# Attention: four of nine key-tile pairs' prob_hi added up on GpSimd, and two maximum banks read by one instruction

## The reference

```
s = einsum('bqkgd,bskd->bkgqs', qblk, k)
p = softmax(s, axis=-1)
return einsum('bkgqs,bskd->bqkgd', p, v)
```

## Time and profile before

| | |
|---|---|
| runs | 1791.49, 1791.6, 1797.52 us; median 1791.6 |
| profiled execution, span | 1794.3 us (its own time isn't given separately) |
| instructions | 22369 |
| attention, first score to last copy | about 322 to 1173 us |

### The profile page before, as it was taken

The page is one execution under the profiler, slowest core; times in us unless marked ns, Lnnn a source line. Parts: engine busy times, 40 slices in busy tenths (PEclk is TensorE's granted clock), DMA queues, the critical chain, the costliest instruction groups (busy, mean ns, idle before and its releaser), DMA issues. The chain is left out here.

```text
span 1794.3 us, 22369 instructions
## 1 busy us (share of the span) xinstructions
PE 1661.6 (93%) x7388; PEld 1314.8 (73%) x7388; DVE 1014.5 (57%) x1451; ACT 832.4 (46%) x1042; POOL 505.2 (28%) x281
## 2 busy tenths in 40 slices
PE   7798885899999999999999999979999969988998
PEld 1487773677777777777777777768888848877886
DVE  1468776687787777778778778530000322254553
ACT  1454532466666766667666666711111132331111
POOL 0032332255445545545444544510000000000000
PEclk9799996799999999999999999989999979999999
DMA  6655445300000000000000000083231035658761
GB/s 223 250 179 169 158 144 133 128 15 23 21 23 16 21 23 15 24 22 15 23 21 16 22 21 23 6 223 124 105 117 47 28 145 199 188 163 231 215 219 74
DMA packets 120466, 171.01 MB, mean 95 GB/s; under 512 B 16065, under 2 KB 82625, under 8 KB 117858
## 3 DMA queue, kind: packets, MB, share of 16 engines
q1 hardware_dynamic: 111874, 147.30, 25.5%
q0 software_dynamic: 8544, 23.07, 4.0%
HBM read 119.89 MB, written 50.46 MB: 95 GB/s over the span
## 5 line engine op out<-in xcount | busy, mean ns | idle before, releaser
L826 DVE TENSOR_REDUCE chunk_max<-max_ps 128x1 f32<-128x512 f32 (+1 forms) x640 | 395.4, 635 | 66.3 <-PE max_ps L892 60.6
L755 POOL TENSOR_TENSOR prob_lo<-prob,prob_hi 128x1024 fp32r<-128x1024 f32 x128 | 306.5, 2395 | 417.3 <-ACT prob L788 417.3
L787 ACT ACTIVATE prob_hi<-s_ps 128x1024 fp32r<-128x1024 f32 x288 | 294.9, 1024 | 229.2 <-PE s_ps L910 229.1
L788 ACT ACTIVATE prob<-s_ps 128x1024 f32<-128x1024 f32 x288 | 293.6, 1019 | 0.0
L892 PE MATMUL max_ps<-k_hi,blk_q_hilo 128*128 128x512 f32 (+1 forms) x640 | 248.1, 390 | 30.3 <-DVE chunk_max L826 12.9
L909 PE MATMUL s_ps<-blk_q_hilo,k_hi 128*128 128x512 f32 x576 | 233.3, 405 | 1.1 <-DVE blk_q_negm L842 0.8
L910 PE MATMUL s_ps<-blk_q_negm,k_lo 65*128 65x512 f32 x576 | 229.3, 398 | 0.0
L930 PE MATMUL hi_ps<-prob_hi,v_hl 128*128 128x512 f32 x576 | 227.6, 395 | 1.5 <-POOL prob_lo L755 1.0
L932 PE MATMUL lo_ps<-prob_lo,v_one 128*128 128x512 f32 x576 | 228.6, 397 | 0.0
L931 PE MATMUL lo_ps<-prob_hi,zero_one 128*128 128x512 f32 x576 | 227.0, 394 | 0.0
L848 DVE TENSOR_TENSOR prob_lo<-prob,prob_hi 128x1024 fp32r<-128x1024 f32 x160 | 197.1, 1232 | 28.4 <-ACT prob L788 28.4
(11 more groups left out here) (169 smaller groups left out, 2508.0 us busy)
## 6 DMA issues: line engine op xcount, KB each, us to landing
tab<-in_dft POOLq DMA_DIRECT2D x16, 1024.0 KB, 7.1
w_mod<-in_w_mod SPq DMA_DIRECT2D x6, 2048.0 KB, 17.4
x<-in_x SPq DMA_DIRECT2D x8, 1024.0 KB, 5.5
h_scratch<-h_hi SPq DMA_DIRECT2D x8, 1024.0 KB, 4.2
h_scratch<-h_lo SPq DMA_DIRECT2D x8, 1024.0 KB, 6.5
q_scratch<-q_hilo SPq DMA_DIRECT2D x16, 512.0 KB, 3.2
blk_q_hilo<-q_scratch SPq DMA_DIRECT2D x32, 256.0 KB, 2.8
hh<-h_scratch SPq DMA_DIRECT2D x4, 2048.0 KB, 10.5
```

Source lines behind the costliest of these rows:

```text
L755: nc.gpsimd.tensor_tensor(prob_lo[slot3(j)][:], prob[slot3(j)][:], prob_hi[slot3(j)][:].bitcast(F32), ALU.subtract).then_inc(s_lo_pool, 1)
L787: nc.scalar.activation(prob_hi[slot3(j)][:], s[:], ACT.Exp)
L788: nc.scalar.activation(prob[slot3(j)][:], s[:], ACT.Exp).then_inc(s_exp, 1)
L826: last = nc.vector.reduce_max(chunk_max[:, qt, kc:kc + 1], bank[:, 0:MAX_CHUNKS[kc]], X_AXIS)
```

## The change

prob_hi of the pairs 0, 1, 3 and 4 is no longer multiplied by zero_one on TensorE. GpSimd adds these four 128 x 1024 tiles up in p_sum (three additions, add), VectorE adds its two halves (fold), ScalarE rounds the result (sum_high), VectorE forms the rest (sum_low), and TensorE multiplies both by zero_one in the last key tile. Exponentials that would overwrite a summed prob_hi wait for its addition. prob_lo is written over prob. Pair 3's lo moves from VectorE to GpSimd, pair 4's from GpSimd to VectorE.

The two maximum banks become one tile max_ps. A use fills both by two matmuls, one reduction reads both, there are 10 uses per block, and s_mfree starts at 1. A use comes after the first scores step and, where MAX_AT has 2, after the first pv step. In the diff, lines with # name the engine; the moved combine (lines 771 and 774 with their waits) is unchanged.

```diff
-MAX_CHUNKS = [512, 512, 512, 512, 256]
-MAX_USES = QB // P * len(MAX_CHUNKS)
-MAX_AT = (4, 4, 3, 4, 3, 2, 0, 0, 0)
-LO_AFTER = (2, 0, 1, 0, 1, 0, 0, 0, 0)
+QT = QB // P
+CHUNK = 512
+CHUNKS = SEQ // CHUNK
+MAX_USES = QT * CHUNKS // 2 + QT // 2
+MAX_AT = (1, 2, 2, 2, 2, 1, 0, 0, 0)
...
-POOL_LO = (0, 2, 4, 6)
+POOL_LO = (0, 2, 3, 6)
+SUMMED = (0, 1, 3, 4)
+FOLD_AT = 6
+ADDS = len(SUMMED) - 1
+
+def max_pair(u):
+    if u < QT * CHUNKS // 2:
+        qt, half = divmod(u, CHUNKS // 2)
+        return [(qt, 2 * half * CHUNK, CHUNK), (qt, (2 * half + 1) * CHUNK, CHUNK)]
+    qt = 2 * (u - QT * CHUNKS // 2)
+    return [(qt, SEQ, CTX), (qt + 1, SEQ, CTX)]
...
-        prob_lo = [sb(f"prob_lo{i}", [P, 2 * QB], F32R) for i in range(3)]
+        prob_lo = [nc.alloc_sbuf_tensor_at(f"prob_lo{i}", [P, 2 * QB], F32R, offset=prob_at + 8 * QB * i)
+                   for i in range(3)]
...
+        p_sum = sb("p_sum", [P, 2 * QB])
+        p_sum_hi = sb("p_sum_hi", [P, QB], F32R)
+        p_sum_lo = sb("p_sum_lo", [P, QB], F32R)
...
-        max_ps = [ps(f"max_ps{i}", [P, QB]) for i in range(2)]
+        max_ps = ps("max_ps", [P, 2, QB])
...
# GpSimd
+            def add(b, i):
+                j = SUMMED[i + 1]
+                if i == 0:
+                    pool.wait_ge(s_sumlo, b + 1)
+                else:
+                    pool.wait_ge(s_acc, b * ADDS + i)
+                pool.wait_ge(s_exp, b * PAIRS + (j + 3))
+                before = prob_hi[slot3(SUMMED[0])] if i == 0 else p_sum
+                nc.gpsimd.tensor_tensor(p_sum[:], before[:].bitcast(F32), prob_hi[slot3(j)][:].bitcast(F32),
+                                        ALU.add).then_inc(s_acc, 1)
...
             def body(b, slot, kvh, next_kvh):
+                add(b, 0)
+                lo(b, 2)
+                lo(b, 3)
+                add(b, 1)
+                add(b, 2)
+                lo(b, 6)
+                if next_kvh is not None:
+                    lo(b + 1, 0)
+                combine(b, slot)
...
# ScalarE, exponentials and body
+                if j >= 3 and j - 3 in SUMMED:
+                    act.wait_ge(s_acc, b * ADDS + max(SUMMED.index(j - 3), 1))
...
+            def sum_high(b):
+                act.wait_ge(s_fold, b + 2)
+                act.wait_ge(s_losum, b + 1)
+                nc.scalar.activation(p_sum_hi[:], p_sum[:, 0:QB], ACT.Copy).then_inc(s_sumhi, 1)
...
+                sum_high(b)
                 if next_kvh is not None:
                     exponentials(b + 1, 1 - slot, 0)
                 evacuate(b, slot)
...
# VectorE
-            dve.sem_inc(s_mfree, 2)
+            dve.sem_inc(s_mfree, 1)
...
             def reduce(b, slot, u):
-                qt, kc = divmod(u, len(MAX_CHUNKS))
-                bank = max_ps[(slot * (MAX_USES + 1) + u) % 2]
+                (qt, key0, width), (qt1, _, _) = max_pair(u)
+                chunk = key0 // CHUNK
+                out = chunk_max[:, qt, chunk:chunk + 2] if qt == qt1 else chunk_max[:, qt:qt + 2, chunk]
                 dve.wait_ge(s_mfull, b * (MAX_USES + 1) + (u + 1))
-                last = nc.vector.reduce_max(chunk_max[:, qt, kc:kc + 1], bank[:, 0:MAX_CHUNKS[kc]], X_AXIS)
+                last = nc.vector.reduce_max(out, max_ps[:, :, 0:width], X_AXIS)
...
+            def fold(b):
+                dve.wait_ge(s_acc, b * ADDS + ADDS)
+                nc.vector.tensor_tensor(p_sum[:, 0:QB], p_sum[:, 0:QB], p_sum[:, QB:2 * QB], ALU.add).then_inc(s_fold, 1)
+
+            def sum_low(b):
+                dve.wait_ge(s_sumhi, b + 1)
+                nc.vector.tensor_tensor(p_sum_lo[:], p_sum[:, 0:QB], p_sum_hi[:].bitcast(F32),
+                                        ALU.subtract).then_inc(s_sumlo, 1)
...
             def body(b, slot, kvh, next_kvh):
+                    if n_max:
+                        reduce(b + 1, 1 - slot, u)
+                    if j + 1 < PAIRS:
+                        lo(b, slot, j + 1)
+                    if n_max == 2:
+                        reduce(b + 1, 1 - slot, u + 1)
...
+                    if j == FOLD_AT:
+                        fold(b)
+                sum_low(b)
                 evacuate(b, slot)
...
# TensorE, max_use, pv and body
                 pe.wait_ge(s_mfree, b * (MAX_USES + 1) + (u + 1))
+                for i, (qt, key0, width) in enumerate(max_pair(u)):
+                    last = nc.tensor.matmul(max_ps[:, i, 0:width], q_hilo[slot][:, qt * P:(qt + 1) * P],
+                                            k.k_hi2[:, kvh, key0:key0 + width], start=True, stop=True)
+                last.then_inc(s_mfull, 1)
...
                 nc.tensor.matmul(hi_ps[:], k.v_hl[:, kt, kvh, :], hi, start=first, stop=final)
-                nc.tensor.matmul(lo_ps[:], k.zero_one[:], hi, start=first, stop=False)
-                last = nc.tensor.matmul(lo_ps[:], v_one[:, kt, kvh, :], lo, start=False, stop=final)
+                if j not in SUMMED:
+                    nc.tensor.matmul(lo_ps[:], k.zero_one[:], hi, start=False, stop=False)
+                if final:
+                    pe.wait_ge(s_sumlo, b + 2)
+                    nc.tensor.matmul(lo_ps[:], k.zero_one[:], p_sum_hi[:], start=False, stop=False)
+                    nc.tensor.matmul(lo_ps[:], k.zero_one[:], p_sum_lo[:], start=False, stop=False)
+                last = nc.tensor.matmul(lo_ps[:], v_one[:, kt, kvh, :], lo, start=first, stop=final)
...
-                        if n < n_max:
+                        if n % 2 == 0 and n // 2 < n_max:
                             max_use(b + 1, 1 - slot, next_kvh, u)
```

More of the change, by code:

```diff
@@ L668, in attention @@
         q_negm = [sb(f"blk_q_negm{i}", [P, QB], F32R) for i in range(2)]
-        chunk_max = sb("chunk_max", [P, QB // P, len(MAX_CHUNKS)])
+        chunk_max = sb("chunk_max", [P, QT, CHUNKS + 1])
         neg_max = sb("neg_max", [P, QB // P])
         diag = sb("diag", [P, QB], F32R)
+        prob_at = nc.sbuf_base
         prob = [sb(f"prob{i}", [P, 2 * QB]) for i in range(3)]
         prob_hi = [sb(f"prob_hi{i}", [P, 2 * QB], F32R) for i in range(3)]
-        prob_lo = [sb(f"prob_lo{i}", [P, 2 * QB], F32R) for i in range(3)]
+        prob_lo = [nc.alloc_sbuf_tensor_at(f"prob_lo{i}", [P, 2 * QB], F32R, offset=prob_at + 8 * QB * i)
+                   for i in range(3)]
         v_one = sb("v_one", [P, KT, HKV, P], F32R)
+        p_sum = sb("p_sum", [P, 2 * QB])
+        p_sum_hi = sb("p_sum_hi", [P, QB], F32R)
+        p_sum_lo = sb("p_sum_lo", [P, QB], F32R)
         part = sb("part", [HD, QB])
@@ L693, in attention @@
         s_part, s_add, s_att = S("v_lo_part_moved"), S("first_att_sum"), S("att_ready")
+        s_acc, s_fold, s_sumhi, s_sumlo = (S("p_hi_added"), S("p_sum_folded"), S("p_sum_hi_ready"),
+                                           S("p_sum_lo_ready"))
         s_st = [S("att_stored0"), S("att_stored1")]
@@ L756, in lo, with combine @@
                                         ALU.subtract).then_inc(s_lo_pool, 1)
[L759 to L767, removed]
+            def add(b, i):
[8 more added lines that the diff above has]
+                                        ALU.add).then_inc(s_acc, 1)
+            def combine(b, slot):
                 pool.wait_ge(s_hisum, b + 2)
@@ L774, in body @@
                 nc.gpsimd.tensor_tensor(att[slot][:], att[slot][:], part[:], ALU.add).then_inc(s_att, 1)
+            for n in range(2):
+                pool.dma_start(k.w_rest_hi[n][:], k.w_rest_v[C_ORDER[n]]).then_inc(k.s_rest_hi[n], 16)
+            lo(0, 0)
+            def body(b, slot, kvh, next_kvh):
+                add(b, 0)
[7 more added lines that the diff above has]
+                combine(b, slot)
             run(pool, body)
@@ L817, in _ @@
         def _(dve):
-            dve.sem_inc(s_mfree, 2)
+            dve.sem_inc(s_mfree, 1)
+            dve.sem_inc(s_fold, 1)
+            dve.sem_inc(s_sumlo, 1)
             nc.vector.memset(hi_sum[:], 0.0).then_inc(s_hisum, 1)
             def reduce(b, slot, u):
-                qt, kc = divmod(u, len(MAX_CHUNKS))
-                bank = max_ps[(slot * (MAX_USES + 1) + u) % 2]
+                (qt, key0, width), (qt1, _, _) = max_pair(u)
+                chunk = key0 // CHUNK
+                out = chunk_max[:, qt, chunk:chunk + 2] if qt == qt1 else chunk_max[:, qt:qt + 2, chunk]
                 dve.wait_ge(s_mfull, b * (MAX_USES + 1) + (u + 1))
-                last = nc.vector.reduce_max(chunk_max[:, qt, kc:kc + 1], bank[:, 0:MAX_CHUNKS[kc]], X_AXIS)
+                last = nc.vector.reduce_max(out, max_ps[:, :, 0:width], X_AXIS)
                 return last.then_inc(s_mfree, 1)
             def negate(b, slot):
-                dve.wait_ge(s_mfree, b * (MAX_USES + 1) + (MAX_USES + 2))
+                dve.wait_ge(s_mfree, b * (MAX_USES + 1) + (MAX_USES + 1))
                 nc.vector.tensor_reduce(neg_max[:], chunk_max[:], X_AXIS, ALU.max, negate=True).then_inc(s_neg, 1)
@@ L838, in max_row @@
             def max_row(b, slot):
```

(13 more changed lines are left out.)

6 lines of the change are left out of this document (removed).

## The result

| | before | changed |
|---|---|---|
| median of all runs | 1793.9 us (4 runs) | 1965.5 us (1957.4, 1957.4, 1973.5, 1975.9) |
| ratio, 95% interval | | 1.0957 (1.0907 to 1.1006) |
| profiled execution, span | 1794.3 us | 1973.5 us, span 1971.6 us |

The change makes the kernel 9.6% slower: 172 us by the medians, 177 us by the spans. The prediction was 1984 us (+192) with 0.90 for slower. Of the 177 us, the blocks of the attention hold nearly all. The period between two hi_sum copies was 26.47 us ((1150.87 - 356.81) / 30) and is 31.76 us ((1321.59 - 368.88) / 30); that is 30 x 5.29 = 159 us. The start of the attention takes 12 us more (368.88 instead of 356.81), the last block 26.8 instead of 21.95 us, 4.8 more; the rest of the kernel 1.7.

What follows compares the result with a forecast made beforehand. TensorE, busy 93%, was taken as the bound. 31 blocks at 5.95 us more give 184, the first maximum 8, the last block 0: +192 on 1791.6, 1984 us; range 1870 to 2075, likeliest case 1925 to 2050.

Steps and rivals of the forecast that it cites:

- Saving on TensorE: Per attention block, four pairs lose two zero_one matmuls each and two come back: 1.39 us less, 44 us in 32 blocks.
- The turn: Maximum tile: fill and reduction alternate, 2.04 us per turn against 1.39 or 1.62 us of cover, 4.7 us stall per block.
- GpSimd's queue: GpSimd in each block: three adds bring 7.2 us more, 20.2 in all; pv(2) waits 1.5 us for lo behind add 0.
- Exclusion: Two-input SBUF work of VectorE and GpSimd can't overlap: 26.8 us per block in series; lo(4) meets add 2.
- the 0.06 us: At lo(4) against add 2 in a block: the closeness of their starts, by which GpSimd was to come first.
- My 31.3 us schedule: Attention block in which VectorE's lo(4) gets in before GpSimd's add 2: it ends at 31.3 us.
- my 33.5 us one: Attention block in which GpSimd's add 2 comes first and lo(4) waits until 16.9: it ends at 33.5 us.
- The middle of the two schedules: Attention block period taken between both orders of lo(4) and add 2: 32.4 us, 5.95 more than 26.45.
- 8 + 6: Start of the attention: 8 us more for the first maximum before the loop, 6 for the first block.
- a rival of 0.06: Attention blocks: stalls lower TensorE's clock to 1.2 GHz for a quarter of each block, +3 x 31, 2077 us; chance 0.06.
- Last block, start: Last block: no maximum for a successor, its 1.4 us saving goes into GpSimd waits, 0; first maximum before the loop: 8 more.
- The signs that I had named: Attention: period 31 to 34 us, reductions about 1.22, 4 or more idle before maximum matmuls, longer lo, 384 zero_one matmuls.

Runs made afterwards that it cites:

- no adds: Changed kernel with GpSimd's three additions left out, so the denominators lack the four pairs: ratio 1.0611, 29.75 us per block.
- banks alone: Kernel before with only the merged maximum tile, one reduction of 1024 elements and s_mfree from 1, no summing: ratio 1.0528, 29.27 us per block.
- wait filled: Changed kernel with six more matmuls that add zero, ahead of pv(2)'s wait: ratio 1.0856, 1942 us, 30.99 us per block.
- add behind diag: Kernel before with pairs 4, 5 and 7 summed, the second addition waiting until VectorE has made the diagonal of maxima: ratio 1.0402, 28.65 us per block.
- combine later: Changed kernel with GpSimd's combine of the last block moved behind lo(b, 3): ratio 1.1228, 2013 us, 33.18 us per block.
- sums alone: Changed kernel's summing with the maximum banks, their 20 uses and s_mfree of the kernel before: ratio 1.0906, 31.54 us per block.

## Why the prediction was right

**Saving on TensorE.** Six matmuls fewer, as said. Their worth was not 1.39 us: left out early with nothing added they gave 0.94 for seven, and under the turns nothing (no adds against banks alone, 0.5 us slower).

**The turn.** 2.04 us predicted, 2.05 measured, reduction 1.22 and 1.22. The run with the banks alone shows it by itself.

**GpSimd's queue.** Adds at 2.38 us alone (2.395 taken). pv(2) was to wait 1.5 us; the distance 671.98 to 673.70 holds 1.5 us above the usual 0.23. The run without adds, in which this wait is gone, and the last block's 5.1 us show it.

**Exclusion.** Right in kind, and the schedule named the place (lo(4) against add 2), but the 0.06 us by which GpSimd was to be first was wrong: an add that waits for the add ahead of it starts 0.16 us late (678.50 after 675.97 + 2.37), so VectorE is first by 0.14 us. My 31.3 us schedule came out at 30.95, my 33.5 us one at 34.0 to 35.2 with a share of 7 in 30 where I had half. That there is a second kind of block at all is not the close race that I had in mind: at clock 1.00 VectorE always comes first (23 of 23, and 30 of 30 with the wait filled), and the long blocks are those in which the clock fell.

**Luck in the number.** The middle of the two schedules, 32.4 us, was 0.6 us over the measured 31.8, about 20 us in all. Had the clock held, the period would have been 31.0 and the change about +150 us (149 by the medians of the run with the filled wait), so the falls of the clock, which the likeliest case didn't have, brought the result nearer to my number. The start came 2 us under my 8 + 6; the last block's 4.8 us and 1.7 us elsewhere go the other way, and leave the 15 between 192 and 177.

**The clock.** I had it as a rival of 0.06 that needs stalls near 4 us, and it was a part of what happened: with waits of 1.3 us and less, but many, the granted clock fell in 7 of 30 blocks (0.89, then 0.68), lo(4) came late and lost its 0.14 us. The filled wait shows that order of cause. It was worth 23 us; the rival's figure, 93 us more than the likeliest case, was too much. What I read wrong in the earlier trace rows was to take one long wait as the measure.

**Last block, start.** The last block was put at 0 and cost 4.8 us: its pv(2) waits 3.4 us for lo(2), which I had not followed there.

```profile
1331.17 0.47 PE L990 MATMUL hi_ps<-prob_hi,v_hl 128*128 128x512 f32 x1 [3.44 <-POOL prob_lo L775]
```

The start, with its first block, was put at 8 + 6 and took 12.

**The signs that I had named.** The period, the length of the reductions, pv(2)'s wait, the 384 zero_one matmuls and VectorE's lo came out as said. Two didn't: GpSimd's lo kept its mean of 2395 ns (its adds paid instead), and TensorE's listed idle time before the maximum matmuls that is put down to chunk_max is 3.1 us per block (75.9 us and 20.4 for the 256-key fills, over 31 blocks) where I had 4 or more.

What stays open: what makes the clock fall in one block and not in the next with the same waits, why the long blocks come in groups, and whether some order of all three engines lets an add in at no cost. No kernel here that computes the whole result beats the kernel before.

## What to carry to other kernels

A buffer pair merged into one saves instructions but makes producer and consumer take turns: add up start-to-start latency, read and hand-back (here 0.34 + 0.43 + 1.22 + 0.05) and compare it with the work that covers it, before counting the matmuls saved. Work moved to an idle engine is free only if its place in that queue has no one waiting behind it, and, for GpSimd, if VectorE has no tensor_tensor or tensor_scalar from SBUF in the same time. Price each meeting at the whole remaining instruction, on the engine that comes second, plus everything queued behind that. In a schedule this tight even removed work can cost time, so judge an edit by which engine comes first at each meeting, not by the sum of busy times. And before two schedules are compared by their mean period, set apart the blocks in which TensorE's clock fell: two of the differences here, 5.1 us for the sums and 1.0 us for the add behind diag, shrink to 3.2 and 0.1.

## What the runs showed of the hardware

- While GpSimd instructions followed each other without waiting for a semaphore, a VectorE instruction with two SBUF inputs didn't get in between them. In the changed kernel's last block a lo of VectorE listed from 1332.63 outlasted the rest of one GpSimd lo *and* a whole add, 4.14 us, and got in where the next add waits for the one ahead of it (a gap of 0.08 us here, 0.16 in the other blocks). With combine later, the same happened in every block (3.56 us at 513.09). GpSimd's two adds, merged, and VectorE's lo:

```profile
1333.33 5.71 POOL L788 TENSOR_TENSOR p_sum<-p_sum,prob_hi 128x1024 f32<-128x1024 f32 x2
```
```profile
1332.63 4.14 DVE L897 TENSOR_TENSOR prob_lo<-prob,prob_hi 128x1024 fp32r<-128x1024 f32 x1 [7.38 <-ACT prob L829]
```

- tensor_scalar from SBUF on VectorE was shut out too: 3.24 us for four, where they took 0.88 in the changed kernel (585.87) and 1.25 in the kernel before (639.83). The Trainium skill, SBUF — State Buffer, section "Who interferes with whom", has tensor_scalar among the operations that can contend with GpSimd in a mode that uses both ports, and this agrees; whether these four ran in that mode no run here shows. Reductions from PSUM never grew (1.23 us at most for 1024 elements, whatever GpSimd did), which fits the rule of the same section of the Trainium skill that tensor_reduce never contends.
- The granted clock fell in stretches where TensorE was busy 2.69 of 4 us with no wait above 1.31 us, stayed at 1.00 in other blocks with the same figures, and stayed at 1.00 in all 30 intervals when six matmuls that add zero filled that wait. At the lower level matmuls of 512 columns start 0.43 us apart instead of 0.23 (371.2 to 373.7 with the sums alone).
- The matmul behind one that had to wait starts 0.31 to 0.34 us after it instead of 0.23: each stall costs 0.1 us beyond itself.
